# A hybrid diffusion layer on one core: token tiles ahead of the adaLN weights, and adaLN rows 4 to 11 moved between the projection tiles

## What is computed

```python
mod = silu(c) @ w_ada + b_ada               # (2 streams, 6 * 1024): c for latent, c_ctx for context tokens
shift1, scale1, gate1, shift2, scale2, gate2 = split(mod, 6)
h = rms(x, norm1_g) * (1 + scale1) + shift1
rq, rk, rv, rg, aq, ak, av, su, g_ret, g_att, g_ssm = split(h @ w_in)
# three branches on h: retention (rq rk rv rg), attention (aq ak av), S5 state space (su)
merged = sigmoid(g_ret) * ret + sigmoid(g_att) * att + sigmoid(g_ssm) * ssm
x = x + gate1 * (merged @ w_out)
h2 = rms(x, norm2_g) * (1 + scale2) + shift2
x = x + gate2 * moe(h2)                      # top-2 of 16 experts
y = rms(x, final_norm_g)
```

## Time and profile before

| | |
|---|---|
| median of 3 runs | 1471.96 us |
| profiled execution, and its span | 1473.11 us, 1471.3 us |
| PE busy | 1273.8 us, 87% of the span |
| DVE, ACT, POOL busy | 39%, 15%, 7% |
| opening, to the first projection matmul | 0 to 63.5 us |
| projections and S5 | 63.5 to 384.6 us |
| retention, attention | to 470.2 us, to 718.5 us |
| merge | 718.5 to 865.2 us |
| output projection with rows 4 to 11 | 865.2 to 974.7 us |
| router, experts, end | 974.7 to 1471.3 us |

### The profile page before, as it was taken

How to read it: one execution, slowest core, us unless ns; L and a number is a source line. 1 busy time by engine, 2 the same in 40 slices (tenths; PEclk the granted TensorE clock), 3 DMA queues, 4 the chain that set the end, 5 groups by cost and what they waited for, 6 DMA issues and landing times. The chain is left out here.

```text
span 1471.3 us, 12983 instructions
## 1 busy us (share of the span) xinstructions
PE 1273.8 (87%) x4938; PEld 657.7 (45%) x4938; DVE 567.2 (39%) x1275; ACT 220.8 (15%) x465; POOL 105.5 (7%) x144
## 2 busy tenths in 40 slices
PE   3799989999986999999999989973599999999950
PEld 1446454556654455555444444443244444444420
DVE  2675848667145644433132332263001011111116
ACT  2111011111432122221000010110001010110002
POOL 2013000010133000000000000002100000000010
PEclk9799999999997999999999999975799999999985
DMA  9324120132202101102123153249298988979524
GB/s 306 139 96 53 58 76 1 58 58 66 82 15 70 61 1 58 58 0 58 57 57 114 58 218 117 104 165 343 65 343 300 344 294 309 333 295 345 210 92 167
DMA packets 93665, 207.58 MB, mean 141 GB/s; under 512 B 10068, under 2 KB 11668, under 8 KB 93604
## 3 DMA queue, kind: packets, MB, share of 16 engines
q1 hardware_dynamic: 82728, 174.48, 33.4%
q0 software_dynamic: 8576, 23.95, 5.7%
q10 hardware_dynamic: 2304, 8.39, 1.4%
HBM read 189.03 MB, written 15.68 MB: 139 GB/s over the span
## 5 line engine op out<-in xcount | busy, mean ns | idle before, releaser
L786 PE MATMUL banks<-wring,HT 128*128 128x512 f32 x480 | 216.1, 599 | 0.8 <-ACTq L354 0.8
L621 PE MATMUL banks<-wring,HT 128*128 128x512 f32 (+1 forms) x480 | 195.2, 568 | 1.1 <-ACT REG L1086 0.5
L916 PE MATMUL banks<-wring,REG 128*128 128x512 f32 x320 | 138.8, 594 | 2.5 <-PE banks L916 1.7
L621 PEld LDWEIGHTS banks<-wring,HT 128*128 128x128 f32 x480 | 92.1, 193 | 99.7 <-issue 96.9
L786 PEld LDWEIGHTS banks<-wring,HT 128*128 128x128 f32 x480 | 89.1, 193 | 97.5 <-issue 96.3
L1003 PE MATMUL banks<-REG 128*128 128x512 f32 x256 | 114.0, 598 | 12.6 <-ACT REG L1254 12.6
L1022 PE MATMUL banks<-wring,HT 128*128 128x512 f32 x256 | 113.1, 600 | 0.9 <-DVE HT L1876 0.9
L1022 PE MATMUL banks<-REG,HT 128*128 128x512 f32 x256 | 111.2, 592 | 0.0
L916 PEld LDWEIGHTS banks<-wring,REG 128*128 128x128 f32 x320 | 60.3, 190 | 80.4 <-issue 79.3
L1003 PEld LDWEIGHTS banks<-REG 128*128 128x128 f32 x256 | 47.3, 190 | 69.8 <-issue 60.6
L1022 PEld LDWEIGHTS banks<-wring,HT 128*128 128x128 f32 x256 | 49.2, 193 | 63.1 <-issue 61.9
(11 more groups left out here) (341 smaller groups left out, 1336.4 us busy)
## 6 DMA issues: line engine op xcount, KB each, us to landing
REG<-w_down SPq DMA_DIRECT2D x16, 2048.0 KB, 12.5
wring<-w_in SPq DMA_DIRECT2D x12, 2048.0 KB, 7.7
wring<-w_gate SPq DMA_DIRECT2D x8, 2048.0 KB, 9.9
wring<-w_up SPq DMA_DIRECT2D x8, 2048.0 KB, 16.3
REG<-w_gate SPq DMA_DIRECT2D x8, 2048.0 KB, 10.0
REG<-w_up SPq DMA_DIRECT2D x8, 2048.0 KB, 16.0
wring<-w_ada SPq DMA_DIRECT2D x7, 2048.0 KB, 15.4
HT<-w_ada SPq DMA_DIRECT2D x4, 2048.0 KB, 12.7
```

The lines of the kernel that those rows point to most:

```text
L621: last = mm(out[:, 0:cols], HT[:, k, P * t:P * t + P], w[:, k, 0:cols], start=k == 0, stop=k == KD - 1)
L786: last = mm(chan.bank(), HT[:, k, P * (i % NT):P * (i % NT) + P], gate[1][:, k, :], start=k == 0, stop=k == KD - 1)
L916: last = mm(out, x[:, k, P * t:P * t + P], w[:, k, :], start=k == 0, stop=k == 3)
```

## The change

In the opening, the five token tiles are loaded ahead of all weights, the four weight blocks of rows 0 to 3 have a slot each (0, 1, 3 and a new slot 8) so that none waits for another, and `upper` (for the router) comes last with a semaphore of its own. Rows are made in the order 0, 2, 1, 3 (`ROW_ORDER`), the turns of the tiles stand between them (`HEAD`), ACT copies half of each turned tile, and four of the eight channel groups are modulated before the last two rows; after the last row DVE and ACT modulate two groups each.

Rows 4 to 11 leave the stage after the merge. PE makes them in the projection stage, between tiles, with `ada_row` as before. DVE adds the four partial sums and the bias on two partitions (`late_row`), and the gain for rows 8 and 9; POOL loads the biases and the norm2 gain into the rows' places and stores each finished row to device memory (`scratch_mod`). Their blocks go through slot 0, the projection blocks between them through slot 1. In the stage after the merge SP reads each pair of rows back, spread over 128 partitions, one transfer of 8 KB per partition. PE's spreading matmuls and ACT's copies of them are gone, and both blocks of `w_out` are loaded before that stage. The gate blocks' slots change parity: the last of the six is now in slot 0, where before it was in slot 1.

```diff
-    blocks = [(w_ada, D, 512 * n, 512) for n in range(4)]
-    blocks += [(w_proj, D, c, 512) for c in (COL_SU, COL_RQ, COL_RK, COL_RV, COL_RG, COL_AQ)] + [(w_proj, D, COL_KV, 256)]
+    ROW_ORDER = (0, 2, 1, 3)
+    blocks = [(w_ada, D, 512 * n, 512) for n in ROW_ORDER]
+    blocks += [in_proj(COL_SU), in_proj(COL_RQ), in_proj(COL_RK), late(4), late(5), late(6), late(7), in_proj(COL_RV), late(8), late(9),
+               in_proj(COL_RG), in_proj(COL_AQ), late(10), late(11), (w_proj, D, COL_KV, 256)]
+    stage_slots = [1, 0, 1, 0, 0, 0, 0, 1, 0, 0, 0, 1, 0, 0, 0]
+    used_later = {6: 9, 11: 13, 15: 17}
...
-    slot_of = [0, 1, 3, 0] + [(n + 1) % 2 for n in range(4, FIRST_MERGE_BLOCK)] + [4, 5, 6, 7] * 2 + [(2, 0, 1)[j % 3] for j in range(10)]
+    slot_of = [0, 1, 3, 8] + stage_slots + [(n + 1) % 2 for n in range(6)] + [4, 5, 6, 7] * 2 + [2, 0]
...
-    blocks += [ada(4), ada(5), (w_out, D, 0, 512), ada(6), ada(7), (w_out, D, 512, 512), ada(8), ada(9), ada(10), ada(11)]
+    blocks += [(w_out, D, 0, 512), (w_out, D, 512, 512)]
...
-             ("F", 1), 3, ("K", 1), 1, ("U", 1), 1, ("V", 1), 10, ("Y", 1), ("out", 1))
+             ("F", 1), 3, ("K", 1), 1, ("U", 1), 1, ("V", 1), 2, ("late", 10), 2, ("late", 11), 6, ("Y", 1), ("out", 1))
...
+    HEAD = (("turn", 0), ("turn", 1), ("row", 0), ("turn", 2), ("columns", 0), ("turn", 3), ("row", 1), ("turn", 4), ("columns", 1),
+            ("row", 2), ("columns", 2), ("row", 3), ("columns", 3))
...
# sync, opening
-        load_x(0)
-        load_block()
-        for t, src in ((ident, "k_ident"), (sel, "k_sel"), (upper, "k_upper")):
+        for t, src in ((ident, "k_ident"), (sel, "k_sel")):
             sp.dma_start(t[:], a[src]).then_inc(consts_in, 16)
+        for t in range(NT):
+            load_x(t)
+        load_block()
...
-        for t in range(1, NT):
-            load_x(t)
-        load_block()
-        load_block()
+        for _ in range(3):
+            load_block()
+        sp.dma_start(upper[:], a["k_upper"]).then_inc(upper_in, 16)
...
# sync, stage after the merge
+        sp.wait_ge(late_out, 16 * 8)
+        def spread_in(j):
+            sp.dma_start(BC2[:, j].rearrange("p s c -> p (s c)"),
+                         scratch_mod[j].rearrange("(o s) c -> o (s c)", o=1).broadcast_to([P, 2 * D])).then_inc(bc_in[j], 16)
+        spread_in(0)
         for t in range(NT):
...
+        for j in (2, 1, 3):
+            spread_in(j)
...
# vector, opening
+            for what, n in HEAD:
+                if what == "turn":
+                    src = vec.take(dve)
+                    vec.give(cp(HT[:, 0:4, P * n:P * n + P], src.rearrange("p (a b) -> p a b", a=4)))
...
+                elif what == "row":
+                    if n >= 2:
+                        dve.wait_ge(full_a, FULL_A_AT_COLUMNS[n - 2])
+                    if n == 2:
+                        dve.wait_ge(free_d, vec.k)
+                        dve.wait_ge(mod_cols, 1)
+                        columns_modulated(range(0, 4))
...
+        def late_row(n):
+            dve.wait_ge(late_in, 16 * 6 if n < 8 else 16 * 10)
+            row = late_slot(n)
+            src = vec.take(dve)
+            if n in (8, 9):
+                done(stt(row, src[0:2], 1.0, row, ALU.add, ALU.add))
+            else:
+                done(tt(row, src[0:2], row, ALU.add))
+            for j in range(1, 3):
+                done(tt(row, src[32 * j:32 * j + 2], row, ALU.add))
+            done(tt(row, src[96:98], row, ALU.add))
+            dve.sem_inc(free_d, 1); vec.k += 1
+            if n in (8, 9):
+                done(tt(row, row, LATE_ROWS[n - 6], ALU.mult))
+            dve.sem_inc(late_ready, 1)
...
# tensor, stage after the merge
-        for step in LAST_ORDER:
-            if step is None:
-                while behind:
-                    spread_one()
-                project_out()
-                continue
-            ada_row(step)
-            behind.append(step)
-            if len(behind) > 1:
-                spread_one()
-        spread_one()
+        project_out()
+        project_out()
```

More of the change, by code:

```diff
@@ L127, in build @@
     SF = r.take(2, 2, GPH)
+    LATE_ROWS = [Region(4 * T + RH * T).take(5, 512, parts=2)[:, j, :] for j in range(5)] + [r.take(512, parts=2)]
     r = Region(OWN)
@@ L647, in modulate @@
             pe.wait_ge(silu_c, 1)
[L648 to L654, removed]
+            for what, n in HEAD:
+                if what == "row":
+                    ada_row(n)
+                elif what == "columns":
+                    ada_columns(n)
+                else:
+                    pe.wait_ge(xn_ready, n + 1)
+                    for half in (1, 0):
+                        transposes((vec, sca)[half], [XN[:, n % 2, P * k:P * k + P] for k in range(4 * half, 4 * half + 4)])
             pe.wait_ge(modulated, 2)
+        def late_row(n):
+            ada_row(n)
         def params(hf):
@@ L1053, in modulate @@
             act.sem_inc(sq_ready, 1)
-            for n in range(4):
+            for what, n in HEAD:
+                if what == "row":
+                    continue
                 src = sca.take(act)
[L1056 to L1059, removed]
+                if what == "turn":
+                    sca.give(A(HT[:, 4:8, P * n:P * n + P], src.rearrange("p (a b) -> p a b", a=4), ACT.Copy))
+                    continue
+                row = ROW_ORDER[n]
+                sca.give(A(MODC[:, row // 2, 4 * (row % 2):4 * (row % 2) + 4, :], src[:, 0:8].rearrange("p (k s) -> p k s", s=2), ACT.Copy))
+                if n % 2:
+                    act.wait_ge(free_a, sca.k)
+                    act.sem_inc(mod_cols, 1)
             for s, cols in enumerate((slice(0, SAMPLE), slice(SAMPLE, T))):
-                for k in range(5, KD):
+                for k in (6, 7):
                     act_going(A(HT[:, k, cols], HT[:, k, cols], ACT.Identity, scale=MODC[:, 1, k, s:s + 1], bias=MODC[:, 0, k, s:s + 1]))
@@ new lines, in modulate @@
+            dve.wait_ge(sq_ready, 1)
+            done(ts(small[:, 8:8 + NT], small[:, 0:NT], 1.0 / D, EPS, ALU.mult, ALU.add))
+            rsqrt(small[:, 16:16 + NT], small[:, 8:8 + NT], small[:, 24:24 + NT])
+            scaled(0)
+            scaled(1)
+            dve.wait_ge(rows_in, 48)
+            for what, n in HEAD:
+                if what == "turn":
+                    src = vec.take(dve)
+                    vec.give(cp(HT[:, 0:4, P * n:P * n + P], src.rearrange("p (a b) -> p a b", a=4)))
+                    if n + 2 < NT:
+                        scaled(n + 2)
+                elif what == "row":
[5 more added lines that the diff above has]
+                        columns_modulated(range(0, 4))
+                    row = ROW_ORDER[n]
+                    mod_row(row, modrow[:, n % 2, :], bias_row[:, row, :], gain_row if row >= 2 else None)
@@ L1741, in _ @@
             return
-        dve.wait_ge(rows_in, 96)
-        fa, rows, half = FULL_A_BEFORE_LAST, 0, 0
-        for step in LAST_ORDER:
-            if step is not None:
-                if rows >= 2:
-                    dve.wait_ge(full_a, fa + 2 * (rows - 1))
-                mod_row(step, modrow2[:, step % 2, :], bias2[:, step - 4, :], gain2 if step in (8, 9) else None)
-                rows += 1
-                continue
+        dve.wait_ge(bc_in[0], 16)
+        dve.wait_ge(x2_in, 16 * NT)
+        for half in range(2):
             ns = slice(512 * half, 512 * half + 512)
-            half += 1
-            dve.wait_ge(bc_ready, 1 + half)
-            dve.wait_ge(x2_in, 16 * NT)
             for t in range(NT):
@@ L1766, in _ @@
         rsqrt(small[:, 16:16 + NT], small[:, 8:8 + NT], small[:, 24:24 + NT])
[L1767 removed]
+        for j in (1, 2, 3):
+            dve.wait_ge(bc_in[j], 16)
         phase_end(dve, 4)
```

124 lines of the change are left out of this document (61 added, 63 removed).

## The result

The changed kernel takes 1460.72 us in the median of four runs (1459.42 to 1463.97), against 1471.99 for the kernel before next to it. The ratio is 0.9917, with a 95% interval of 0.990 to 0.9934: 10 to 15 us faster. 1462.4 was forecast.

The account below looks back on a forecast made before the run. TensorE was taken as the bound, busy nine tenths or more nearly everywhere. Seven terms summed to -9.6 us, taking the profiled 1473.11 to 1463.5, or 1462.4 as a median; range 1452 to 1471.

Parts of the forecast that it names:

- Step 1: Opening: tokens loaded first and rows and turns reordered let the modulation end earlier; -6.0 us, range 3 to 10 gained.
- Step 2: Rows 4, 5, 6 ahead of Y of half 0: row time plus 0.6 us waits at rows 5 and 6; +5.3 us.
- Step 3: Row 7 between Y and the output turns: TensorE's row, then VectorE's additions ahead of the parameter copies; +2.2 us.
- Step 4: Rows 8 and 9 ahead of F of half 1: row time, VectorE's delayed multiplications and a lower clock; +14.5 us.
- 5 rows 10, 11: Rows 10 and 11 between tiles ahead of the second Y: only TensorE's time, 2 x 2.5; +5.0 us.
- step 6: Start of the merge: w_ret_out asked for later because of the gate slots' parity, plus clock; +3.5 us, range 2 to 6.
- Step 7: Output projection stage: TensorE starts at once, with spread and token loads hidden behind its tiles; -34.1 us.
- Rival B: Rows 5 and 6: blocks through slot 0 land in 15.4 us instead of 7.7; 1477.8 us, chance 0.08.
- Rival A: Rows cost only TensorE time, F is not held, and the opening runs at the high clock; 1450.5 us, chance 0.13.
- Rival C: Last stage starves: spread and X2 land 25 us late, 11 past the cover; 1473 us, no change, chance 0.05.
- Rival D: Opening gains nothing, TensorE and VectorE taking as long as before in another order; 1468.4 us, chance 0.12.

Follow-up runs that it names:

- one-block run: Changed kernel with rows 5 and 6 multiplied from row 4's block, their own not loaded; one run, first Y 41.25 us behind the RK tile.
- the other spreads first: Changed kernel with three other spreads (3 MB) ahead of gate1's spread and the tokens in the output projection's stage; one run, 1456.93 us.
- row 7 moved: Changed kernel with swapped gate slots, VectorE's rows 8 and 9 behind F, and row 7 behind half 1's parameter turns; 1446.06 us, ratio 0.9828.

## Why the prediction was right, step by step

| step | forecast | measured | read from |
|---|---|---|---|
| 1 opening | -6.0 | -8.1 | first RK tile 163.06 to 154.98 |
| 2 rows 4 to 6 | +5.3 | +6.4 | RK tile to first Y, 38.0 to 44.45 |
| 3 row 7 | +2.2 | +0.6 | Y to first RV tile, 21.08 to 21.68 |
| 4 rows 8, 9 | +14.5 | +15.3 | RV tile to the end of the three tiles, +14.2 and 21.88 - 20.77 |
| 5 rows 10, 11 | +5.0 | +4.8 | 19.13 at Y less 14.3 at K |
| 6 w_ret_out | +3.5 | +3.9 | 19.13 at Y to 23.01 behind the merge |
| 7 output projection | -34.1 | -34.1 | 23.01 to 11.1 earlier |
| rest | 0 | +1.8 | 11.1 to 9.3 |
| sum | -9.6 | -9.3 | spans |

The waits were the ones forecast, each at the place named; what the prediction had wrong are sizes, above all of the clock. That the sum fits to 0.3 is partly luck: steps 1 and 3 came out 3.7 better, and 2, 4, 6 and the rest 4.1 worse. The spans are also those of one execution, the slowest of four. The medians moved by 11.3, 1.7 more than forecast; the steps without the rest add up to -11.1, which would fit, but no other execution has a profile.

Step 1. The range between the two clocks was right (45 to 49), and the last row's matmuls end at 46.5: the four rows took 2.36, 1.92, 3.49 and 3.26, at granted clocks of 1.00, 1.00, 0.54 and 0.57. So the rows ended 5.4 earlier, where 4.6 of the 6.0 was for them. The tail from there to the first tile shrank by 2.4 (11.5 to 9.1), where 1.4 was taken; both parts were sized too low, the tail by more.

Step 2. The waits were 1.75 and 0.87, not 0.6 each: the block was taken to land in 7.7, and w_ada blocks landed in 8.5 in the median:

```profile
wring<-w_in SPq DMA_DIRECT2D x12, 2048.0 KB, 8.2
wring<-w_ada SPq DMA_DIRECT2D x10, 2048.0 KB, 8.5
...
wring<-w_ret_out SPq DMA_DIRECT2D x2, 1024.0 KB, 5.7
```

Rival B needed 12.5. The one-block run shows that these waits are all there is.

Step 3. VectorE's row 7 did hold the parameter turns, for 1.14 us. The step was small for two reasons. Y itself ran faster: it is over 14.2 us after its start, where it took 15.9. No wait for the scan stood ahead of it any more, and with that wait went the low clock behind it: the four us from the start of Y had 0.61 before and 1.00 in the changed kernel. The prediction had priced the wait and not the clock. And row 7 fills a place where TensorE had been idle. Before, it waited 1.16 for ScalarE ahead of the outputs' turns:

```profile
215.84 1.10 PE L744 MATMUL banks<-REG 64*80 64x128 f32 x16
218.10 0.78 PE L761 MATMUL banks<-ident,REG 80*128 80x80 f32 x8 [1.16 <-ACT REG L1092]
```

In the changed kernel it waits 0.33 there, behind the row:

```profile
213.66 1.92 PE L629 MATMUL banks<-wring,cS 128*32 128x512 f32 x16
215.91 0.74 PE L788 MATMUL banks<-ident,REG 80*128 80x80 f32 x8 [0.33 <-PE banks L629]
```

So it is -1.6 for Y, +1.9 for the row, -0.8 at the outputs' turns and +1.1 at the parameters' turns.

Step 4. Two waits of 4.05 and 3.96 were forecast as some 4 us ahead of each half, and stood where the prediction put them. The kernel with VectorE's order changed is the proof: it takes back 9.9 and leaves 5.5. Rival A gave 1450.5 for rows that cost TensorE alone, with 2.4 of it from a faster opening; that kernel makes the rows so, and takes 1450.78.

Steps 4 and 6, the clock. Behind the second wait at F the last 16 turns ran at a granted clock of 0.50 and took 3.56 (273.43 to 276.99), where the same 16 took 2.3 at 1.00 before (from this row to 263.80):

```profile
261.50 1.06 PE L597 MATMUL banks<-ident,REG 128*128 128x128 f32 x8 [0.29 <-ACT REG L1071]
```

That is 1.3 lost; the three tiles behind lost another 1.1 (21.88 at 0.95 for 20.77 at 1.00), and the 40 matmuls of the merge 1.7 (19.10 at 0.91 for 17.43 at 1.00). In all it is 4.0, where 1.5 was taken. The first 16 turns of F were slow too (0.57), but that cost nothing, since TensorE had to wait for VectorE's second half in any case. All these losses vanish together with their waits in the experiments. Of the three waits only the merge's was for a transfer. By place, the path paid nothing behind the first wait, 2.4 behind the second and 1.7 at the merge. In step 6 two errors cancelled: the wait grew by 2.1 (0.85 to 2.99) where 2.9 was forecast, and the clock took 1.7 where 0.6 was. Waits of 1.75 and 0.87 at rows 5 and 6, for transfers too, cost no clock: the row and the tile behind each took 1.92 or 1.93 and 7.11 or 7.10, at 1.00.

Step 7. The cover was 27.6 us from the stage's start, and VectorE had its tokens 11.5 into it, about the 13 that were forecast. The run with the other spreads first moved this to 18.8 at no cost to the stage. Rival C was far off.

Rival D (an opening that gains nothing) falls with the opening alone, ratio 0.9949.

## What to carry to other kernels

When work is moved between the tiles of a busy engine, cost it on every engine that handles it, and look above all at what stands behind it in the order of the helper: two rows of 2.5 us on TensorE cost 15 us because VectorE had them ahead of the multiplications for which TensorE was due, and putting them behind gave 10 us back. Changing how many blocks pass through two slots also changes which slot the last one has, and with it whether the next stage's first weights can be loaded early; that cost 4 us here and one expression to mend.

## What was not expected of the hardware

The opening alone spread more from run to run than the kernel before did on the same chip: 1460.67 to 1466.85, beside 1470.84 to 1471.88. That the new opening is the cause is not shown: two other kernels that have it spread by 1.4 and 2.7 us on that chip, and the kernel before spread by 7.6 on the other.

The profiles show places where executions differ. In the opening the second row took 1.92 at a granted clock of 1.00 in the changed kernel and 3.50 at 0.53 in the opening alone: the four rows took 2.36, 1.92, 3.49 and 3.26 in the one and 1.93, 3.50, 3.55 and 2.95 in the other, and the first projection tile came between 53.9 and 56.7 in eight kernels' profiles with this opening. The 128 short matmuls of K of half 0 took 8.83 in one profile (row 7 moved), at 0.81, and 7.16 in the others, at 1.00. The first 32 expert matmuls took between 15.4 (at 0.91, the other spreads first) and 17.1 (at 0.82, the changed kernel). And the wait for the gathered tokens ahead of the experts was between 29.2 and 31.2 us in nine profiles, with the same instructions ahead of it; the 34.55 of the one-block kernel can't be set beside them, since its rows 5 and 6 hold other values and its tokens may be sorted otherwise. That these places make up the whole spread of the times is not shown, since each kernel has one profiled execution.
